# Attention beside gate products: the products go unit by unit, with the weight splits between their steps

## The reference, cut to what matters

```python
h = rmsnorm(x, norm1_g)
u, v_a, q, k, v_b = split(h @ w_in)
y_a = chunked_spatial_gating(u, v_a, ...)
# 8 heads of causal attention, each with two softmaxes a = p0 - lam * p1
sc = q @ k.T * scale + alibi          # per head, 4 blocks of 128 queries
a = softmax(sc[0]) - lam * softmax(sc[1])
o = rmsnorm(a @ v_b) * (1 - lam_init)
gates = sigmoid(h @ w_gate + b_gate)
g_a, g_b = split(gates)
merged = g_a * (y_a @ w_up_a) + g_b * (y_b @ w_up_b)
x = x + merged @ w_out
```

## Time and profile before

| | us |
|---|---|
| median of 3 runs (lowest, highest) | 1773.82 (1771.23, 1778.03) |
| the profiled execution | 1772.76 |
| its span | 1770.7 |
| TensorE busy in it | 1523.5 (86%) |
| VectorE, ScalarE busy | 948.3 (54%), 714.9 (40%) |

### The profile page before, as it was taken

One profiled execution on the slowest core, in us unless ns is written; L12 is line 12 of the kernel. 1 busy time (PEld: TensorE's weight loads), 2 busy tenths in 40 slices (PEclk: granted clock), 3 DMA queues, 4 the chain that ended last, 5 costly groups with the idle time before them and its releaser, 6 DMA issues.

```text
span 1770.7 us, 17596 instructions
## 1 busy us (share of the span) xinstructions
PE 1523.5 (86%) x7159; PEld 1147.0 (65%) x7159; DVE 948.3 (54%) x1301; ACT 714.9 (40%) x1043; POOL 68.2 (4%) x80
## 2 busy tenths in 40 slices
PE   5999997798786963899999991989697899999999
PEld 4888775586565842555555551868585877678887
DVE  3444246623763445788888874675545535321334
ACT  4333334424443220666666662244322215652231
POOL 1000000000000000111011101000000000000000
PEclk9999998998997986899999996999897988999999
DMA  6422221122104430999999984220101003002241
GB/s 197 168 96 75 96 73 66 68 75 72 70 26 161 152 119 23 307 327 340 331 336 335 329 294 156 72 71 26 47 1 48 1 24 119 1 1 72 95 143 48
DMA packets 80348, 224.01 MB, mean 127 GB/s; under 512 B 9044, under 2 KB 10182, under 8 KB 76167
## 3 DMA queue, kind: packets, MB, share of 16 engines
q1 hardware_dynamic: 71558, 193.73, 32.3%
q0 software_dynamic: 6144, 20.71, 3.5%
q10 hardware_dynamic: 2560, 8.39, 1.3%
HBM read 200.00 MB, written 22.81 MB: 126 GB/s over the span
## 4 chain that ended last, share of the span: by engine, by line
PE 59%; DVE 25%; ACT 11%; DMA 2%; issue 2%; SPq 1%; POOL 0%; DVEq 0%; POOLq 0%; ACTq 0%
PE PS L502 14%; PE PS L504 14%; PE PS L503 14%; DVE wlo L1152 7%; DVE htlo L1152 5%; PE PS L928 4%; ACT whi L1950 3%; PE PS L499 3%; DVE ylo L1152 2%; ACT work L1950 2%; PE PS L1077 2%; ACT yhi L1950 2%; PE PS L1068 1%; ACT hthi L1950 1%; DVE work L1561 1%
## 5 line engine op out<-in xcount | busy, mean ns | idle before, releaser
L1152 DVE TENSOR_TENSOR wlo<-raw,whi 128x2048 fp32r<-128x2048 f32 x74 | 169.1, 2291 | 356.3 <-ACT whi L1950 356.3
L1950 ACT ACTIVATE whi<-raw 128x2048 fp32r<-128x2048 f32 x74 | 141.2, 1912 | 334.9 <-PE PS L504 333.5
L499 PE MATMUL PS<-consts,work 128*128 128x128 f32 (+1 forms) x652 | 100.7, 298 | 125.9 <-DVE work L1178 53.2
L502 PE MATMUL PS<-whi,hthi 128*128 128x512 f32 x480 | 200.1, 417 | 9.2 <-ACT work L1950 6.4
L502 PE MATMUL PS<-hthi,whi 128*128 128x512 f32 x480 | 198.3, 413 | 5.1 <-ACT scratch L1950 2.8
L503 PE MATMUL PS<-wlo,hthi 128*128 128x512 f32 x480 | 190.9, 398 | 0.0
L504 PE MATMUL PS<-whi,htlo 128*128 128x512 f32 x480 | 190.8, 398 | 0.0
L504 PE MATMUL PS<-hthi,wlo 128*128 128x512 f32 x480 | 190.0, 396 | 0.0
L503 PE MATMUL PS<-htlo,whi 128*128 128x512 f32 x480 | 189.5, 395 | 0.0
L499 PEld LDWEIGHTS PS<-consts,work 128*128 128x128 f32 (+1 forms) x652 | 85.2, 182 | 155.1 <-DVE work L1178 54.4
L1950 ACT ACTIVATE work<-PS 128x512 f32<-128x512 f32 (+3 forms) x204 | 103.3, 531 | 88.6 <-PE PS L992 51.2
(11 more groups left out here) (320 smaller groups left out, 2600.3 us busy)
## 6 DMA issues: line engine op xcount, KB each, us to landing
raw<-in_w_in SPq DMA_DIRECT2D x44, 1024.0 KB
raw<-in_w SPq DMA_DIRECT2D x80, 512.0 KB
scratch<-in_w SPq DMA_DIRECT2D x48, 512.0 KB
raw<-in_w SPq DMA_DIRECT2D x19, 1024.0 KB
scratch<-in_w SPq DMA_DIRECT2D x13, 1024.0 KB
raw<-in_w_gate SPq DMA_DIRECT2D x8, 1024.0 KB
raw<-in_w_out SPq DMA_DIRECT2D x8, 1024.0 KB
y_scratch<-work ACTq DMA_DIRECT2D x32, 256.0 KB, 7.1
```

Of the source, the lines that this page charges most:

```text
L499: return e.transpose(o, i, ident[0:n, 0:n])
L502: e.matmul(o, lh, rh, start=start, stop=False)
L1152: tt(lo, raw_place(j), as_f32(hi), SUB).then_inc(*ve.mark("lo", j))
L1950: return e.activation(o, i, f, bias=bias, scale=scale)
```

## The change

Gate products are made unit by unit: `part` runs all four column blocks over unit 0, which leaves four banks open and frees the unit's slot after 16 steps, and then over unit 1. The splits stand between the steps, at 18, 34, 50 and 66, two steps behind the end of a unit. Steps 64 to 79 are the first half of the next product: q's second block in pass 0, `ub`'s first product in pass 1, whose heads 0 to 3 are ready by then. `product` then starts at its second unit (`first`). Two steps are taken ahead of the loop, and the last five iterations have three places each.

The first gate is not written to memory: ScalarE copies it to the upper halves of `yhi` and `ylo` (`y_plain`), whose heads 4 to 7 are filled only in pass 1. Its sigmoids and its products with `merged` stand at the start of pass 1's projections, and pass 1's heads wait for them before they are written there. The second gate still goes through memory; it is loaded over the turned q and k after the last scores, in two parts, and only its eight sigmoids stand behind the pass. x's copy for the residual, which shares space with it, waits for the last merged sum. The code of `product` was merged with the new `part`; where it runs by itself its instructions are the same and in the same order.

In the first fence is TensorE in pass 0 before, from the scores of iteration 8 (128 wide) into iteration 9; `hthi,whi` is a gate step's first matmul, `work` at L658 scores, `consts,scratch` the turning of weights, `work,scratch` the product with v.

```diff
-    gate_a = W[:, 2:4, :].rearrange("p a n -> p (a n)").rearrange("p (k n) -> p k n", k=KD)
+    gate_a = [y_plain[:, k // HB, HB + k % HB, :] for k in range(KD)]
+    gate_b = W[:, 1:3, :].rearrange("p a n -> p (a n)").rearrange("p (k n) -> p k n", k=KD)
...
+    AHEAD = 2
+    SPLITS = (18, 34, 50, 66)
+    GATED = 2 * KD * HB
-    GAP = 6
...
-        def product(name, b, turned, hi, lo, ready=None, by_k=None):
...
-        def product_in_steps(name, b, ready):
...
+        def part(name, b, kh, turned, hi, lo, ready=None, by_k=None):
             j0, n = unit[name, b]
+            j, last = j0 + kh, kh == n - 1
+            wh, wl = halves(j)
             for c in range(HB):
+                cols, key = slice(c * P, c * P + P), (name, b, c)
+                if kh == 0:
+                    bank.take(key)
+                ps = PS[:, bank.of[key], :]
+                for k in range(HB):
+                    kk = kh * HB + k
+                    on.wait_ge(*ve["lo", j])
...
+                    if k == HB - 1 and last:
                         m.then_inc(*pe.mark(*key))
                         bank.filled(key)
...
+                    elif k == HB - 1 and c == HB - 1:
                         m.then_inc(*pe.mark("unit", j))
+                    yield
+
+        def product(name, b, turned, hi, lo, ready=None, by_k=None, first=0):
+            for kh in range(first, unit[name, b][1]):
+                for _ in part(name, b, kh, turned, hi, lo, ready, by_k):
+                    pass
...
         def beside_attention(half):
             for b in range(2):
-                yield from product_in_steps(("ga", "gb")[half], b, h_ready)
-                for _ in range(GAP):
-                    yield
+                for kh in range(2):
+                    yield from part(("ga", "gb")[half], b, kh, True, hthi, htlo, h_ready)
+            if half == 0:
+                yield from part("q", 1, 0, False, hthi, htlo, h_ready)
+            else:
+                yield from part("ub", 0, 0, True, yhi, ylo, by_k=yb_ready)
 
         for half in range(2):
-            product("q", half, False, hthi, htlo, h_ready)
+            product("q", half, False, hthi, htlo, h_ready, first=half)
...
+            for _ in range(AHEAD):
+                next(beside)
             for n in range(STEPS + 5):
...
-                next(beside, None)
+                if n < STEPS:
+                    next(beside, None)
...
-            product("ub", b, True, yhi, ylo, by_k=lambda k: ve["out", "yb", k])
+            product("ub", b, True, yhi, ylo, by_k=yb_ready, first=1 - b)
...
         def beside_attention(half):
-            for b in range(2):
-                for c in range(HB):
-                    for kk in range(KD):
-                        yield
-                for step in range(GAP):
-                    if step in (0, 2):
-                        split()
-                    yield
+            for step in range(GATED + KD * 2):
+                if step in SPLITS:
+                    split()
+                yield
...
+            if half:
+                for k in range(KD):
+                    on.wait_ge(*ac["gate a", k])
+                    tt(mg[:, k, :], mg[:, k, :], gate_a[k], MUL).then_inc(*ve.mark())
+                ve.also("first merged 1")
...
+            if b:
+                on.wait_ge(*ve["first merged 1"])
             act(yhi[:, hh, :], inside("yb", hh), ACT.Copy, scale=sg8).then_inc(*ac.mark("yb hi", hh))
 
-        def gate_chunk(half, b, c):
+        def gate_chunk(half, k):
+            name, b, c = ("ga", "gb")[half], k // HB, k % HB
             on.wait_ge(*pe[name, b, c])
-            if half or k > 1:
-                on.wait_ge(*gate_put[k % 2][half * KD + k - 2])
+            if half == 0:
+                on.wait_ge(*pe["ua", 1, HB - 1])
+                act(gate_a[k], inside(name, b, c), ACT.Copy).then_inc(*ac.mark("out", name, b, c))
+                return
...
+                at = step % (KD * HB) - HB * HB
+                if step < GATED and at >= 0 and at % HB == HB - 1:
+                    gate_chunk(half, step // (KD * HB) * HB + at // HB)
...
+            if half:
+                for k in range(KD):
+                    act(gate_a[k], gate_a[k], ACT.Sigmoid, bias=bg[:, k:k + 1]).then_inc(*ac.mark("gate a", k))
...
-        on.wait_ge(*gate_got["all"])
         for k in range(KD):
-            act(gate_a[:, k, :], gate_a[:, k, :], ACT.Sigmoid, bias=bg[:, k:k + 1]).then_inc(*ac.mark("gate a", k))
-        for k in range(KD):
-            act(gate[:, k, :], gate[:, k, :], ACT.Sigmoid, bias=bg[:, KD + k:KD + k + 1]).then_inc(*ac.mark())
+            on.wait_ge(*gate_got[k // HB][k // HB])
+            act(gate_b[:, k, :], gate_b[:, k, :], ACT.Sigmoid, bias=bg[:, KD + k:KD + k + 1]).then_inc(
+                *ac.mark("merged", "gate", k))
...
         for j in range(NR + NS, unit["ub", 0][0] + NR):
             load(j)
+        on.wait_ge(*pe["scores", 1, STEPS - 1, 1])
+        for b in range(2):
+            on.wait_ge(*gate_put[0][HB * b + 2])
+            on.wait_ge(*gate_put[1][HB * b + 3])
+            e.dma_start(gate_b[:, HB * b:HB * b + HB, :], gate_dram[HB * b:HB * b + HB].rearrange(
+                "k p n -> p k n")).then_inc(*gate_got[b].mark(b))
         on.wait_ge(*ve["attention"])
         on.wait_ge(*pe["yb", 7])
...
-        e.dma_start(gate_a, gate_dram[0].rearrange("k p n -> p k n")).then_inc(*gate_got.mark("first"))
-        e.dma_start(gate, gate_dram[1].rearrange("k p n -> p k n")).then_inc(*gate_got.mark("all"))
...
-        on.wait_ge(*ve["first merged 1"])
+        on.wait_ge(*ve["merged", "sum", KD - 1])
         e.dma_start(xw, xv).then_inc(*xw_got.mark("all"))
```

More of the change, by code:

```diff
@@ new lines, in part @@
+                cols, key = slice(c * P, c * P + P), (name, b, c)
[5 more added lines that the diff above has]
+                    on.wait_ge(*ve["lo", j])
+                    if ready:
+                        on.wait_ge(*ready)
+                    if kh == 0 and k == 0:
+                        on.wait_ge(*emptied(bank.before[key]))
+                    if by_k:
+                        on.wait_ge(*by_k(kk))
+                    if turned:
+                        m = passes(ps, wh[:, k, cols], wl[:, k, cols], hi[:, kk, :], lo[:, kk, :],
+                                   kk == 0, kk == n * HB - 1)
+                    else:
+                        m = passes(ps, hi[:, kk, cols], lo[:, kk, cols], wh[:, k, :], wl[:, k, :],
+                                   kk == 0, kk == n * HB - 1)
+                    if k == HB - 1 and last:
@@ L1360, in vector, with merge_second @@
         ve.also("attention")
-        def merge_second(name, halves, event):
+        def merge_second(name, halves, event, gate):
             def low_part(k):
@@ L1383, in merge_second @@
                         low_part(k)
-        for k in range(KD):
-            on.wait_ge(*ac["gate a", k])
-            tt(mg[:, k, :], mg[:, k, :], gate_a[:, k, :], MUL).then_inc(*ve.mark())
-        ve.also("first merged 1")
-        merge_second("ub", 2, "merged")
+        merge_second("ub", 2, "merged", gate_b)
         ve.also("merge end")
@@ L2458, in scalar @@
         gates("g2b", bg2, KD, [ve["first merged"]])
-        ac.also("merged2", "gate")
+        for k in range(KD):
+            ac.also("merged2", "gate", k)
         merge_second(1, "merged2", pe["g2b", 1, HB - 1])
```

97 lines of the change are left out of this document (23 added, 74 removed).

## The result

The changed kernel takes 1717.05 us (median of 4 runs, 1715.52 to 1726.43), the kernel before took 1775.92 beside it (4 runs, 1771.23 to 1784.81): a ratio of 0.967, 95% interval 0.962 to 0.973. 1726 was forecast, 1712 to 1746 the range. The execution profiled took 1715.52 us, its span 1713.7: 57.0 less than before.

The account below looks back on a forecast made before the run. Waits on a chain, not a full engine, were taken to bound the attention passes and what follows them. Gains of 16.8 + 27.2 + 3.4 = 47.4 us off 1772.76 gave 1725.4, with 1.06 added 1726 us; range 1712 to 1746, chance 0.68.

Parts of the forecast that it names:

- Start: Start of each pass: the 3.1 us wait stays and two gate steps of 0.74 us each follow, 4.6 us.
- Iterations 0 to 2: First iterations of a pass: as before, slow clock included, 13.4 us in pass 0 and 14.4 in pass 1.
- Heads: Iterations 3 to 15, three heads: 20.4 us plus 1.1 for a split, 21.5 each, 64.5 for three; bounds 19.0 and 24.1.
- End of a pass: Iteration 15 to the last turning: 19.4 us of work and about 2 us of waiting, 21.4 us.
- Behind the passes: After pass 0, q's remaining half takes 10.9 us (pass 0 and q gain 16.8); first gate's sigmoids and v's split stay hidden.
- Tail: Behind pass 1: second `ub` product starts 11.2 us after the pass; from pass 1 to there 27.2 us gained.
- the 288 matmuls: Matmuls from the second `ub` product on: 65.5 us in place of 69.0 without the wait ahead, put down as 3.4 gained.
- VectorE's pace (1): Heads in the passes: each split costs its full 2.25 us plus 1.5 of waiting, 24.1 a head, 1742 us; chance 0.15.
- `wo`'s last unit (2): Load behind x's copy: split ends 68.9 us after pass 1, 3.2 late, clock some 2 more, 1731 us; chance 0.08.
- Bank shortage (3): PSUM banks in the passes: TensorE waits between groups at the lower clock, 0.68 us more a step, 1835 us; chance 0.03.
- The psum-queue rule: Skill rule: short idles while turning through PSUM banks swing the clock; passes would pay the bank shortage price, part or whole.
- "It does more" (4): Heads in the passes: every split hidden and the 1.5 us of waiting gone, 19.0 us a head, 1711 us; chance 0.06.

## Why the prediction came out as it did

**The bound.** Right: the paired splits, the gates' way through memory and the serial halves were what the three stages lost. Undoing any one of the three costs 29 us by the medians and 22 to 27 in the stretch. They sum to 74 there, against the 57.3 of the whole change, so what one is worth depends on the other two.

**Start: right in pass 0.** 3.2 us of wait and two steps, 4.8 for the 4.6 of the sum. In pass 1 the two steps ran at half the clock (0.77 and 0.63 us rows), 6.1.

**Iterations 0 to 2: mis-sized.** "As now", slow clock included, gave 13.4 and 14.4; they took 10.9 and 12.2. I had kept the slow clock of the stretch without asking what stands behind the wait. All profiles together settle the size: from the end of k's turning to the scores of iteration 3, the sixteen passes with two steps ahead behind a wait of 3.1 or 3.2 us take 15.6 to 18.4 us, 17.0 in the mean, and the six without steps ahead 16.2 to 17.5, 16.8 in the mean. So the two steps, for which the sum had 1.5 us on top of the old stretch, cost 0.2. The changed kernel's 15.6 and 18.2 stand near both ends of that range and make up for each other. Which level follows the wait is not the pass's doing: in pass 0 the two steps ran at full speed in four profiles and at half in four, in pass 1 at half in all eight. What decides it is open.

**Heads: the step that failed most, 3.0 us a pass.** I put 20.4 for a head without a split and 1.1 for the split. Leaving VectorE's part out gives 18.3, 20.5 and 20.5, and the split costs 0.9, 0.7 and 0.7. So for the two later heads the base was right and only the split 0.4 too dear; 2.4 of the 3.0 us are the first head's, whose base was 2.1 too high. That base was read from the old order, where each gate block is copied just ahead of the exponentials. `AHEAD` moves that copy to another place, and the kernel before with two steps ahead has the 18.3 us too; I had priced those two steps as TensorE's alone. That the first head has no head to normalise, and so no 1.3 us wait, was visible in the order and not used. The bounds, 19.0 and 24.1, held the 20.5 of the mean, but 19.0 is not TensorE's own work in every head: the first took 18.2 us without splits, TensorE busy all the time. The scores of iterations 3 and 15, forecast 64 to 66 us apart, stood 61.5 apart.

**End of a pass: right.** 21.2 in both for 21.4, and the run without the half product, at 21.0, shows it to be near the chain's length.

**Behind the passes: right.** q's half 10.9 us in one piece. The sigmoids began 11.2 us behind q, ended at 16.2, the split was through VectorE at 20.4 and k's matmuls at 22.0 (9.7 plus a table load, 16.0, 20.1 and 21.8 forecast). The 1.4 us between q and pass 1 that I did not count is the clock, 1.00 after and 0.97 before, and luck: behind the same 3.20 us wait ahead of v, at which nothing was changed, matmuls soon stand 0.43 us apart before and stay at 0.23 after, and the other kernels show now the one, now the other.

**Tail: right.** 11.4 us from the end of the pass to the second `ub` product, 11.2 forecast. (69.0 less 65.5 for the 288 matmuls is 3.5 us, not the 3.4 of the sum; 2.9 came.) Behind the table load the first sigmoid starts 0.01 us after its end. The drain that the Trainium skill adds ("ScalarE: Activation LUTs", What ACT_TABLE_LOAD costs) is not seen here either; it would have come on top of the 0.32 us wait.

**Rivals.** VectorE's pace (1): wrong for one split a head, true for two. `wo`'s last unit (2): it did not come late. TensorE works 66.01 of the 66.10 us in which it is wanted, and the unit's low part is done 60.8 us after the pass, 62 forecast. (The rival's own terms add up to 67.9 us, not 68.9.) Bank shortage (3): none with eight, 0.8 us a pass with seven. The psum-queue rule of the Trainium skill ("TensorE: Matmul & The Clock Gate", A second HAM failure mode: psum-queue depth-cycling) finds no support at waits of 1.3 us, once a head, at a clock of 1.00; at waits of 2.3 us and more the lower level did follow in some heads of other runs (last section). "It does more" (4): its 19.0 us a head came only in the first.

The profiled execution, 1715.52 us, was 9.8 us under the 1725.4 of the sum: 6.1 from heads, 4.7 from iterations 0 to 2, 1.4 from the middle and 0.3 from the ends of the passes, less 1.7 at the starts, 0.7 in the tail and the 288 matmuls, and 0.4 outside the stages. The median of the runs is 1.5 us above that execution.

## What to carry to other kernels

Where several engines count the steps of a side job in one loop, shifting it moves every engine's share of it, and what counts is what queues behind a share that waits: two steps cost TensorE 4 us (2.6 in the stretch), and ScalarE's and VectorE's order behind them 35 (31 in the stretch). Price a piece of side work against the slack of the engine that holds it: the first split cost a third of its length, the second all of it. A base taken from the old order is only good if the order around it stays.

## What the runs showed of the chip

A wait of 3.20 us ahead of the same two gate steps was followed by matmuls 0.24 us apart in pass 0 (clock 1.00) and by matmuls 0.43 us apart in pass 1 (0.81 over the stretch) of the changed kernel. Across the kernels it is not a matter of the pass: with splits in pairs, without the next half and with gates by memory pass 0 has 0.43 too. The wait of 0.89 us left both at 0.24.

Inside the passes the same holds. With VectorE's part of the splits done twice, waits of 3.06 us in the first heads were followed by the lower level (0.93 over the head); of the four waits of 2.80 us in the other heads one was (0.93, in pass 1) and three were not (1.00). With six steps ahead a wait of 2.38 us stands in two heads of pass 0 at 0.93, and in a head of pass 1 at 1.00. The length of a wait alone does not tell the clock behind it.

Where the clock is 1.00, the same stretch of instructions repeats to 0.03 us over executions and kernels (heads of 19.11 to 19.14, 21.18 to 21.20 and 21.18 to 21.20 us in five kernels), so a difference of 0.1 us in such a stretch can be read.
